# Second layer: a gate unit between the router's two token tiles, and the input turned into four free banks

## The reference, cut to what matters

```
for i in range(2):                              # first block
    proj = x @ w_in[i]                          # queries, keys, values, latents, gates
    merged = sigmoid(g_na) * (o_na @ w_na_o[i]) + sigmoid(g_mla) * (o_mla @ w_mla_o[i])
    x = layer_norm(ALPHA * x + merged @ w_out[i])
    if i == 0:
        f = swiglu(x, ffn_w1, ffn_w3, ffn_w2)
    else:                                       # 8 experts, the best 2 for each token
        logits = x @ w_router + b_router
        top_vals, top_idx = top_k(logits, 2);  gates = softmax(top_vals)
        f = sum over e of gates[:, e] * swiglu(x, w1[e], w3[e], w2[e])   # 1024 -> 3584 -> 1024
    ple = sigmoid(x @ w_ple_gate[i]) * (p[i] @ w_ple[i])
    x = layer_norm(ALPHA * x + f + ple)
x = hybrid_layer(x)                             # second block
```

## Time and profile before

| | us |
|---|---|
| median of 3 runs | 2018.38 |
| lowest and highest | 2018.35, 2020.46 |
| profiled execution: span | 2018.5 |
| TensorE busy | 1982.4 (98%) |
| VectorE busy | 1603.9 (79%) |
| ScalarE busy | 1017.1 (50%) |
| GpSimd busy | 59.0 (3%) |
| HBM read | 528.02 MB, 273 GB/s over the span |

### The profile page before, as it was taken

How to read it: one execution, slowest core, us unless ns; L and a number is a source line. 1 busy time by engine, 2 the same in 40 slices (tenths; PEclk the granted TensorE clock), 3 DMA queues, 4 the chain that set the end, 5 groups by cost and what they waited for, 6 DMA issues and landing times.

```text
span 2018.5 us, 27225 instructions
## 1 busy us (share of the span) xinstructions
PE 1982.4 (98%) x10728; PEld 1676.7 (83%) x10728; DVE 1603.9 (79%) x1618; ACT 1017.1 (50%) x1047; POOL 59.0 (3%) x53
## 2 busy tenths in 40 slices
PE   8999999999999999999999999999999998999999
PEld 7988788889988778888888888888888887868887
DVE  3676688886666698888888888888888975668987
ACT  0264110021453377777777777777777753472000
POOL 0110100000000200000000000000000000100000
PEclk9999999999999899999999999999999999999999
DMA  9643588753634589999999999999999985445650
GB/s 322 195 164 110 181 296 315 271 165 122 211 124 178 222 298 384 380 380 370 384 384 377 384 380 379 373 385 384 382 384 371 408 287 164 135 126 167 205 175 37
DMA packets 184217, 553.15 MB, mean 274 GB/s; under 512 B 9296, under 2 KB 112080, under 8 KB 140864
## 3 DMA queue, kind: packets, MB, share of 16 engines
q1 hardware_dynamic: 175296, 517.55, 69.7%
q10 hardware_dynamic: 6912, 25.02, 3.2%
q0 software_dynamic: 1920, 9.34, 1.2%
HBM read 528.02 MB, written 23.59 MB: 273 GB/s over the span
## 4 chain that ended last, share of the span: by engine, by line
PE 93%; DVE 3%; ACT 3%; issue 1%; DMA 0%; DVEq 0%; ACTq 0%; SPq 0%
PE act_ps L1190 30%; PE dve_ps L1215 15%; PE act_ps L1040 9%; PE job_ps L1144 6%; PE act_ps L1112 4%; PE dve_ps L1112 4%; PE dve_ps L916 4%; PE dve_ps L1040 2%; PE act_ps L1087 2%; PE job_ps L1067 2%; PE act_ps L1111 2%; PE dve_ps L1111 2%; PE act_ps L916 1%; PE job_ps L1198 1%; PE job_ps L967 1%
## 5 line engine op out<-in xcount | busy, mean ns | idle before, releaser
L2482 DVE TENSOR_TENSOR weights_rest<-weight_ring,expert_short 128x2048 fp32r<-128x2048 f32 x336 | 762.9, 2289 | 103.2 <-ACT expert_short L1781 102.6
L1781 ACT ACTIVATE expert_short<-weight_ring 128x2048 fp32r<-128x2048 f32 x336 | 641.0, 1916 | 109.9 <-PE act_ps L1190 74.1
L1190 PE MATMUL act_ps<-expert_short,tokens_short 128*128 128x512 f32 x896 | 354.2, 395 | 3.9 <-ACT arena_o L1798 2.0
L1190 PE MATMUL act_ps<-expert_short,tokens_rest 128*128 128x512 f32 x896 | 349.2, 390 | 0.0
L1190 PE MATMUL act_ps<-weights_rest,tokens_short 128*128 128x512 f32 x896 | 349.1, 390 | 0.0
L1190 PEld LDWEIGHTS act_ps<-expert_short,tokens_short 128*128 128x128 f32 x896 | 168.2, 188 | 38.7 <-DVE weights_rest L2482 3.2
L1190 PEld LDWEIGHTS act_ps<-expert_short,tokens_rest 128*128 128x128 f32 x896 | 168.2, 188 | 36.3
L1190 PEld LDWEIGHTS act_ps<-weights_rest,tokens_short 128*128 128x128 f32 x896 | 168.4, 188 | 33.6
L1767 ACT ACTIVATE arena_mla<-arena_mla 128x512 f32<-128x512 f32 x22 | 14.0, 634 | 298.4 <-DVE arena_mla L2415 298.4
L2402 DVE TENSOR_TENSOR weights_rest<-weight_ring,ffn_weights_short 128x2048 fp32r<-128x2048 f32 x66 | 151.3, 2292 | 2.2
L1215 PE MATMUL dve_ps<-expert_short,hidden_short 128*128 128x512 f32 x440 | 137.1, 393 | 0.0
(11 more groups left out here) (421 smaller groups left out, 3518.3 us busy)
## 6 DMA issues: line engine op xcount, KB each, us to landing
weight_ring<-in_moe_w SPq DMA_DIRECT2D x336, 1024.0 KB, 6.8
weight_ring<-in_w_in SPq DMA_DIRECT2D x43, 1024.0 KB, 8.0
weight_ring<-in_ffn_w SPq DMA_DIRECT2D x32, 1024.0 KB, 7.8
weight_ring<-in_w_out SPq DMA_DIRECT2D x12, 1024.0 KB, 6.8
weight_ring<-in_w_gate SPq DMA_DIRECT2D x11, 1024.0 KB, 5.3
weight_ring<-in_w_up SPq DMA_DIRECT2D x11, 1024.0 KB, 8.1
weight_ring<-in_w_down SPq DMA_DIRECT2D x10, 1024.0 KB, 7.0
weight_ring<-in_w_ple_gate SPq DMA_DIRECT2D x8, 1024.0 KB, 6.2
```

The source lines that it names most:

```text
L1190: m = nc.tensor.matmul(bank[0:CAP, :], a[:, 4 * c + k, :], w[:, k, :], start=(c == k == i == 0), stop=(c == 1 and k == 3 and i == 2))
L1781: nc.scalar.activation(shorts[u % SHORTS][:, :], ring[:, slot, half], ACT.Copy).then_inc(moe_w_short, 1)
L2482: V.tensor_tensor(ring_lo[slot][:, half], ring[:, slot, half], shorts[u % SHORTS][:, :], ALU.subtract)\
```

## The change

In the second layer only, the order on TensorE becomes: logits of token tile 0; the first 12 products of gate unit 4; logits of token tile 1; the sixteen transposes of x; the other 12 products of unit 4; places; units 5 to 7. `beside` is now a pair of callbacks, one behind each half of unit 4. The transposes of x write to the four banks `acc_ps`, one group each, without a wait, and count up a semaphore of their own, `x_turned`. ScalarE reads them from there and counts up `x_tok_copied`, on which its own scaled copy and GpSimd's scatters wait instead of on the count of ScalarE's tiles. The four tiles drop out of the plan ("D" instead of "DAAAA"), and so does VectorE's wait for them in `router()`. The first layer still turns x through ScalarE's banks.

```diff
--- before.py
+++ after.py
@@ -437,6 +437,7 @@
         scores_ready, max_ready, exp_done = sem("scores_ready"), sem("max_ready"), sem("exp_done")
         probs_ready, probsT_ready, probsT_copied = sem("probs_ready"), sem("probsT_ready"), sem("probsT_copied")
         pv_ready, out_copied = sem("pv_ready"), sem("out_copied")
+        x_turned, x_tok_copied = sem("x_turned"), sem("x_tok_copied")
         routed, exp_gap, sel_ready, overflow_ready = sem("routed"), sem("exp_gap"), sem("sel_ready"), sem("overflow_ready")
         moe_here = [sem(f"moe_here{i}") for i in range(SLOTS)]
         rows_clear, rows_cleared, rows_known, rows_sent = (
@@ -552,7 +553,7 @@
             out += [(halves(panel(t["w_out"][l], 512 * i, 512 * (i + 1))), "UU") for i in range(2)]
             out += [(ple_block(l), "AAAA")]
             if l:
-                out += [(None, "D" + "A" * 4)]
+                out += [(None, "D")]
             out += [(halves(panel(t["w_ple_gate"][l], 512 * i, 512 * (i + 1))), "AA") for i in range(2)]
             if not l:
                 out += [(None, "AAAA")]
@@ -569,7 +570,6 @@
         queries_at.append(loads_of(plan) + len(lat_blocks(1)))
         plan += layer_plan(1)
         ple_block_at.append(loads_of(plan) - 3)
-        router_at = len(plan) - 3
         plan += [(None, "D")]
         before_moe = loads_of(plan)
         plan += [(None, "A")]
@@ -590,8 +590,6 @@
             if dmas:
                 tiles_before.append((n.a, n.d))
             n.a, n.d, n.w, n.m, n.u = [at + what.count(kind) for at, kind in zip((n.a, n.d, n.w, n.m, n.u), "ADWMU")]
-            if at == router_at:
-                x_tok_at = n.a
             if dmas:
                 blocks.append((dmas, {"A": (act_tile_ready, n.a), "D": (dve_tile_ready, n.d),
                                       "W": (down_used, n.w), "M": (mix_ready, n.m), "U": (merged_unit_used, n.u)}[what[-1]]))
@@ -832,7 +830,7 @@
                             .then_inc(y_picked, 16)
 
             pool.wait_ge(rows_cleared, ROWS_CLEAR)
-            pool.wait_ge(act_tile_done, x_tok_at)
+            pool.wait_ge(x_tok_copied, 2 * QT)
             pool.wait_ge(rows_known, 1)
             for k in range(2):
                 for i in range(QT):
@@ -1088,20 +1086,20 @@
                                                      start=(c == k == p == 0), stop=(c == 1 and k == 3 and p == 2))
                         if c:
                             m.then_inc(act_tile_ready, 1)
-                        if beside and i == 4 and r == 0:
-                            beside()
+                        if beside and i == 4:
+                            beside[r]()
                     if c == 0:
                         m.then_inc(ple_unit_used, 1)
                 n.block += 2
 
-            def turn_x(l):
+            def turn_x(banks, done):
 
                 for i in range(QT):
                     for half in range(2):
-                        bank = act_bank()
+                        bank = banks(2 * i + half)
                         for k in range(4):
                             m = nc.tensor.transpose(bank[:, k * P:(k + 1) * P], x[:, 4 * half + k, i * P:(i + 1) * P], const("ident"))
-                        m.then_inc(act_tile_ready, 1)
+                        m.then_inc(done, 1)
 
             def half_terms(bank, w, at, k):
 
@@ -1421,18 +1419,21 @@
                 embedding(2, 4)
                 if l == 0:
                     ple_rows(l, lambda k: (ffn_x_split, k + 1))
-                    turn_x(l)
+                    turn_x(lambda i: act_bank(), act_tile_ready)
                     swiglu(FT, None)
                     pe.wait_ge(act_tile_done, n.a)
                     turn_rows(2 * l + 1, act_ps + job_ps[0:2])
                 else:
                     pe.wait_ge(x_ready, DT * (2 * l + 1))
                     bank = dve_bank()
-                    for i in range(QT):
-                        m = product(bank[:, 8 * i:8 * i + 8], token_tiles(x, i),
-                                    [param("router_w")[:, 8 * k:8 * k + 8] for k in range(DT)])
-                    m.then_inc(dve_tile_ready, 1)
-                    turn_x(l)
+
+                    def logits_of(i):
+                        return product(bank[:, 8 * i:8 * i + 8], token_tiles(x, i),
+                                       [param("router_w")[:, 8 * k:8 * k + 8] for k in range(DT)])
+
+                    def last_logits():
+                        logits_of(1).then_inc(dve_tile_ready, 1)
+                        turn_x(lambda i: acc_ps[i], x_turned)
 
                     def places():
                         pe.wait_ge(sel_ready, 1)
@@ -1441,7 +1442,8 @@
                         product(bank[:, 8:16], [const("ones"), const("before")], [sel[:, i, 0:EXPERTS] for i in range(QT)])
                         product(bank[:, 16:24], [const("ones")] * QT, [sel[:, i, 0:EXPERTS] for i in range(QT)])\
                             .then_inc(dve_tile_ready, 1)
-                    ple_rows(l, lambda k: (ffn_x_split, DT * l + k + 1), places)
+                    logits_of(0)
+                    ple_rows(l, lambda k: (ffn_x_split, DT * l + k + 1), (last_logits, places))
                     pe.wait_ge(overflow_ready, 1)
                     more = pe.value_load(overflow[0:1, 0:1], min_val=0, max_val=1)
                     experts(0)
@@ -1959,10 +1961,12 @@
                 else:
                     for i in range(QT):
                         for half in range(2):
-                            read(x_tok[:, i, half * 512:(half + 1) * 512], ACT.Copy, width=512)
+                            act.wait_ge(x_turned, 2 * i + half + 1)
+                            nc.scalar.activation(x_tok[:, i, half * 512:(half + 1) * 512], acc_ps[2 * i + half][:, :], ACT.Copy)\
+                                .then_inc(x_tok_copied, 1)
                     act.wait_ge(routed, 1)
                     nc.scalar.activation(route[:, 2:4], route[:, 0:2], ACT.Exp).then_inc(exp_gap, 1)
-                    act.wait_ge(act_tile_done, n.a)
+                    act.wait_ge(x_tok_copied, 2 * QT)
                     nc.scalar.activation(z_rows, x_tok, ACT.Copy, scale=ALPHA).then_inc(rows_scaled, 1)
                     for j in range(4):
                         gate_rows(j)
@@ -2459,7 +2463,6 @@
                         m = V.tensor_scalar(onehot[:, k, i, :], const("iota8"), at, None, ALU.is_equal)
                 step(m)
                 V.tensor_tensor(sel[:, :, :], onehot[:, 0], onehot[:, 1], ALU.add).then_inc(sel_ready, 1)
-                act_tiles(4)
                 bank = ready()
                 V.tensor_tensor(pos, tiles(bank[:, 0:16], QT), tiles(const("first_row"), QT), ALU.add)
                 V.tensor_reduce(route[:, 12:13], bank[:, 16:24], AX_X, ALU.max).then_inc(dve_tile_done, 1)
```

## The result

| | before | after |
|---|---|---|
| median of six runs, us | 2018.37 | 2024.89 |
| lowest and highest, us | 2016.37, 2020.46 | 2022.72, 2026.33 |
| profiled execution: time, us | not shown | 2025.30 |
| profiled execution: span, us | 2018.5 | 2023.5 |

The ratio of the medians is 1.003, with a 95% interval of 1.002 to 1.004. The forecast was 2016.9, and its range ended at 2020.0.

The account below looks back on a forecast made before the run. TensorE was taken to bound the kernel, with the first expert's rows next: −2.36 at the tokens, +0.9 for the clock, 0 for issues and DMA, −1.5 us in sum, giving 2016.9 us, range 2014.4 to 2020.0.

Parts of the forecast that it names:

- Free banks: TensorE's sixteen transposes of x, written to four free banks without waits: 1.76 us instead of 4.67, gain 2.91 us.
- The clock: First gate unit's products: full clock would give back 1.91 us; 0.9 us was taken as lost, bounds nothing to 3.82.
- TensorE's sum: At full clock, everything behind the first gate unit 4.82 us earlier; TensorE ready for the tokens at 705.30.
- VectorE behind the places: The weight split follows routing at once, done at 693.1 before TensorE needs it at 693.4; cost nothing.
- Where it would be decided: At the first expert's rows, landing at 707.76 and limiting the gain at the tokens to 2.36 us.
- DMA: Scatters beside earlier weight loads: −1.7 to +2.8 us; with issues −1.7 to +4.4, taken as 0.
- GpSimd's issues: Four scatter issues now beside VectorE's splits: bounds nothing to +1.6 us; with DMA taken as 0.
- Behind the tokens: First expert: TensorE idles about 2.4 us ahead; a clock fall is absorbed by the 2.04 us wait for ScalarE.
- my reading of the time: Whole kernel: median 2018.38 taken as 0.1 us under the profiled span of 2018.5, turning 2017.0 into 2016.9.
- The clock falls twice: Rival: both narrow pieces drop TensorE's clock, each block of 12 takes 4.64 us; slower, 2020.3 us; chance 0.15.
- The rows keep up: Rival: scatters and read finish 2.4 us sooner against the places, so TensorE's whole 4.82 us arrives; 2013.6 us; chance 0.07.

Follow-up runs that it names:

- e5: Changed kernel with SyncE's sixth and seventh expert block loads both held until the first expert's rows have landed; 2015.71 us, ratio to before 0.9983.
- e6: Changed kernel with both weight loads held until the first rows landed, and VectorE's splits held until the four scatters landed; 2025.45 us, one run.
- e3: Changed kernel with the seventh expert block load held until the first rows landed, the sixth only until the scatters landed; 2020.21 us, ratio to before 1.0004.
- e2: Changed kernel with only SyncE's last load, the seventh expert block, held until the first expert's rows have landed; 2019.65 us, ratio to before 1.0002.
- e9: Changed kernel with 15 added products of 256 columns, results unused, on TensorE before its wait for the rows; 2023.19 us, ratio to before 1.0025.
- e12: Kernel before the change, with both weight loads held until the first expert's rows have landed; 2018.03 us, ratio to before 0.9999.
- e7: Changed kernel with 30 added products of 256 columns, results thrown away, on TensorE before its wait for the rows; 2034.88 us, ratio to before 1.0081.
- e8: Kernel before the change, with only the last load held until the first expert's rows have landed; 2018.66 us, ratio to before 1.0000.
- e1: The changed kernel run again without any edit; 2024.08 us, ratio to before 1.0026.
- e4: Free banks alone: changed kernel with both tiles' logits and transposes ahead of the gate unit, places behind its first 12 products; 2017.15 us, ratio to before 0.9993.
- e10: Free banks alone, both tiles' logits together as before, with both weight loads held until the first rows landed; 2018.38 us, ratio to before 0.9995.
- e11: Changed kernel with both weight loads held until the first rows landed, run a second time on another chip; 2016.03 us, ratio to before 0.9985.

## Why the prediction was wrong

**What held.** *Free banks*: sixteen transposes, no waits, 1.80 us, where 1.76 was worked out. *The clock*: one block of 12 ran mostly at half clock, 4.44 us, so 1.7 us were lost of which I had taken 0.9; but the logits of both tiles, now at full clock, took 3.63 us instead of 4.39, and at the places the account closes: from the first logit to their end it is 13.69 us instead of 14.88, a gain of 1.19, and the working had 2.09 − 0.9 = 1.19. That they agree is luck: a fall that cost 0.8 us more than taken and logits 0.8 us shorter than taken cancel. *TensorE's sum*: the last gate product ended 31.2 us behind the first logit; 706.2 − 675.19 = 31.0 was forecast, and e5 has its tokens at 30.98. *VectorE behind the places* cost nothing, as said: the split followed routing at once, at 689.70. *Where it would be decided*: at the rows, as said.

**The step that failed is "DMA"**, together with "GpSimd's issues" the term that I put at 0 with bounds of −1.7 and +4.4. From the places' end to the landing of the rows, where the tokens now start, it is 24.97 us, and before it was 19.78: +5.2, outside both bounds. To the tokens before it was 20.05. In parts, from the rows of both traces:

- first issue behind the places: 1.91 us against 2.00, −0.1;
- from the first scatter's issue to the end of the fourth's: 8.12 us against 6.59, +1.5. This is the upper bound of the issues (+1.6), which I had set aside. e6 shows the cause: with VectorE still, the same four take 4.87 us from first to last.
- from the end of the last issue to the read's: 7.32 us against 6.59, +0.7. The first pair of loads, issued at 693.84 instead of 698.37, meets three scatters. The median landing rose from 4.5 to 8.5 us. e3 and e5 have 2.6 us there, without these loads.
- the read: 7.6 us against 4.6, +3.0. **This was in neither bound.** I followed the first pair of loads past the scatters and stopped; I moved the read by the same amount as the scatters and kept its 4.6 us. Before, the last gate unit was through 5.1 us behind the read's issue, so its loads (710.31) came when the read was down. Counted from the first logit, the change made TensorE 3.9 us earlier there and the read 1.0 us later, which put the one on the other. e2 takes it out alone: 3.5 us of read, 4.3 with the clock.

The 0.27 us by which the rows had been ahead of TensorE are used up by it. The sum at the tokens, with the second decimals, is −1.19 − 0.09 + 1.53 + 0.73 + 3.02 − 0.27 = +3.73 us.

The range was also narrower than these bounds: with the +4.4 beside the 0.9 for the clock it would have ended at 2018.4 − 2.36 + 0.9 + 4.4 = 2021.3, and it was drawn at 2020.0, just short of the rival. Both lie under what was measured. (Its lower end works out at 2014.3, not 2014.4.)

**The second miss is "Behind the tokens".** I had the fall of the clock in TensorE's wait slow the first units and be absorbed by the wait for ScalarE behind the fourth. That part held. The wait, 2.04 us before, is 0.65 in the changed kernel and 0.17 in e2, where the clock fell just behind the tokens and cost 0.06 us in all (23.40 against 23.34):

```profile
730.65 0.49 PE L1188 MATMUL act_ps<-expert_short,tokens_short 128*128 128x512 f32 x1 [0.65 <-ACT arena_o L1800]
...
725.81 0.49 PE L1190 MATMUL act_ps<-expert_short,tokens_short 128*128 128x512 f32 x1 [0.17 <-ACT arena_o L1802]
```

What I missed is the size of the wait, 7.49 us against 2.4. In it the clock was down before the tokens came, so they took 1.97 us instead of 1.03, and everything behind waits for them. From tokens to first result it is 24.27 us instead of 23.34, +0.9, and e9 gets 0.86 back by keeping TensorE busy. 3.73 + 0.93 = 4.66 us.

**The third is my reading of the time.** I set the profiled span of 2018.5 beside the median of 2018.38. In the runs that have both, time less span is 1.8 us, so the profiled execution of before was one of its longer ones, at some 2020.3, and a usual one has a span of 2016.4 as in e12. That can explain a part of how a stretch that costs 4.3 to 4.66 us shows as 5.4 to 6.5 in the medians: the clock of the norm at 448 us was at its half level in eight of the nine traces of the changed order (their logits start at 674.3 to 675.1), in one of two with the banks alone and in one of three of the order before. Whether the change causes that or it fell so by chance isn't settled: nothing ahead of 448 us is changed except where the instructions lie. But all nine versions of the changed order lose 0.9 to 1.9 us more, or gain less, than their stretch says (e7 after its stop of 3.66 and what goes with it, 5.9 us, is taken off), and e8 and e12 don't (−0.1 and −0.4). In e5 a stretch 3.95 us shorter gives 3.0 us of time. So a cost of the change outside its stretch is left open here.

**The rivals.** "The clock falls twice" gave 2020.3 on the slower side, by another cause; the clock did fall twice, but the second time in the wait. "The rows keep up" gave −4.82 us. With both loads held it happened, less the 0.9 us of the clock: −3.95 in the stretch of e5. I gave it 0.07 for want of room in the DMA engines. The room was there, but taken by loads that nobody needed yet: I never asked whether they could come later.

**What slows an issue, and what slows the read.** The fourth scatter was issued from 696.28 to 698.30, in 2.02 us, and VectorE's timeline of the changed kernel shows no cast beside it:

```profile
693.91 1.23 DVE L2384 CAST ffn_weights_short<-weight_ring 128x2048 fp32r<-128x2048 f32 x1 [0.66 <-PE act_ps L1085]
695.18 2.29 DVE L2386 TENSOR_TENSOR weights_rest<-weight_ring,ffn_weights_short 128x2048 fp32r<-128x2048 f32 x1
697.39 0.68 DVE L2688 TENSOR_TENSOR probs<-probs,arena_mla 128x512 f32<-128x512 f32 x1
698.11 0.69 DVE L2689 TENSOR_TENSOR pre_norm<-pre_norm,probs 128x512 f32<-128x512 f32 x1
```

So operations of two tensors slow it too, and I had counted the casts' 1.23 us alone (twice that is 2.5, and doesn't give the +1.6 that I put beside it). The Trainium skill (SBUF — State Buffer, "Who interferes with whom") has that rule beside the one which the prediction drew on: a VectorE instruction with two inputs in SBUF contends with a GpSimd instruction that reads SBUF; it infers, however, that this spares the writing of descriptors. The slow issue beside operations of two tensors alone agrees with the rule if the issue of a scatter is such an instruction, which no run here shows, and not with the inference if it is only the writing of descriptors.

For the read, the DMA view of the changed kernel from 705 to 714 us (first what moved, then by queue: packets, MB, share; then each issue with its median from issue to landing):

```profile
DMA packets 431, 2.62 MB, mean 291 GB/s; under 512 B 47, under 2 KB 47, under 8 KB 175
...
q1 hardware_dynamic: 287, 2.10, 61.5%
q0 software_dynamic: 144, 0.52, 14.4%
...
weight_ring<-in_moe_w SPq DMA_DIRECT2D x2, 1024.0 KB, 6.9
arena_mla<-expert_rows_in POOLq DMA_DIRECT2D x1, 512.0 KB, 7.6
```

The read was issued first and is a fifth of the bytes, and yet it landed behind one of the two loads (they took 5.5 and 8.3 us). The Trainium skill (DMA: Bandwidth & Descriptors, "Queues, rings and completion order") lets each DMA engine take packets in turn from the queues that have work. By that the read's 144 packets would have gone out with as many of the loads', 0.52 + 1.05 = 1.57 MB; at the 0.40 MB/us of the earlier trace rows that is 3.9 us, and with the 2.2 us that the read takes alone beyond its bytes (3.5 − 1.3) about 6.1, an estimate. It took 6.9 to 8.5 (6.9 in e7 and e9, 7.2 in e1, 7.6 in the changed kernel, 8.5 in e3). So the trace agrees that it slows, and has it slower than fair turns would; why isn't settled.

## What to carry to other kernels

When a change lets one engine run ahead of another, list every transfer that its progress sets free and lay it beside every small transfer on the other path, the last one included: a read of 0.5 MB that the next stage waits for costs 3 to 5 us more when two loads of 1 MB start with it. If the loads aren't urgent, let them wait for the small transfer's landing, and release them by that landing and not by what releases the read itself (e3 against e5). Compare traces from a common point close ahead of the change, since chance ahead of it can be as large as the effect.

## What the runs showed of the hardware

- The read of the first expert's rows: 3.4 to 4.0 us with no load beside it, 4.4 to 4.6 with a pair issued some 7 us ahead of it, 6.9 to 8.5 with two loads of 1 MB starting at the same time.
- A scatter of 128 rows takes 0.96 to 1.05 us to issue with VectorE still (e6) and 1.54 to 2.04 beside its work in the changed order; with no weight loads beside them the scatters had landed 2.6 to 3.4 us after the last issue, with a pair of loads beside them after 6.6 to 7.5.
- TensorE's clock fell to 1.2 GHz at about 676.8 (0.85 over 675.10 to 677.50), 0.3 us behind a narrow piece of 1.95 us (16 records of 8 columns) and with the engine counted busy throughout; the sixteen of the second tile, behind wide products, took 1.68 us and didn't drop it. In e9 products whose result nobody reads kept it at 1.00 through the wait.
- One short wait in a norm, 2.4 us, drops the clock in some traces and not in others, though all is the same up to there, and moves the logits by some 2 us. Around a wait of 2.03 to 2.08 us in the first expert it fell in three traces (e4, e7, e10) and stayed at 1.00 in seven (before, e5, e6, e8, e9, e11, e12).
- A fall of the clock behind the tokens was taken in by a later wait and cost 0.06 us (e2); one ahead of them cost 0.86 to 0.93 us (e9 against e1, and the changed kernel).
